# Sample-state products on column quarters and 32-row groups, with attention gates projected ahead of and among sample pairs

## The reference, cut to what matters

```
y_off = einsum('bclgn,bcgrpn,bclgr->bclgrp', cm, h_in, exp(la))      # C x incoming state
states = einsum('bclgn,bclgr,bclgrp->bcgrpn', bm, to_end, xdt)       # B x (decayed x dt)
h = h * chunk_decay + states                                         # new state
out = rms_norm((y_diag + y_off + d_skip * xs) * silu(z_s), norm_g)   # state-space group
o = sum over branches of sigmoid(gate) * branch output
y_att = rms_norm(o * silu(z_a), att_norm_g)                          # attention group
x + gate * (concat(out, y_att) @ w_out), then a final rms_norm
```

## Time and profile before

| what | value |
|---|---|
| median of 3 executions | 985.8 us (982.7 to 985.88) |
| profiled execution, its own time | 985.73 us |
| its span | 983.9 us |
| mean granted TensorE clock | 0.978 |
| TensorE products busy | 924.6 us (94%) |
| VectorE busy | 490.6 us (50%) |
| ScalarE busy | 343.1 us (35%) |
| GpSimd busy | 158.8 us (16%) |
| chain that ended last | PE 77%, DVE 9%, ACT 5%, issue 4%, DMA 4% |

### The profile page before, as it was taken

The page is one execution under the profiler, slowest core; times in us unless marked ns, Lnnn a source line. Parts: engine busy times, 40 slices in busy tenths (PEclk is TensorE's granted clock), DMA queues, the critical chain, the costliest instruction groups (busy, mean ns, idle before and its releaser), DMA issues.

```text
span 983.9 us, 13227 instructions
## 1 busy us (share of the span) xinstructions
PE 924.6 (94%) x5187; PEld 573.6 (58%) x5187; DVE 490.6 (50%) x961; ACT 343.1 (35%) x698; POOL 158.8 (16%) x125
## 2 busy tenths in 40 slices
PE   2999999999999999997989888899999999999995
PEld 1454764465566567776555545556666666666762
DVE  1141301135353445558623445886767666676553
ACT  3140000201011224443132334675665546544531
POOL 1003491000000144435211000900000000000000
PEclk9999999979999989998999999999999999999998
DMA  8926435123120000300832134400000000011011
GB/s 280 352 75 258 171 123 204 44 84 114 57 87 1 5 1 1 86 1 1 310 133 92 47 127 149 129 2 22 12 23 23 22 23 23 1 44 44 1 44 65
DMA packets 36567, 80.67 MB, mean 82 GB/s; under 512 B 3044, under 2 KB 17580, under 8 KB 35162
## 3 DMA queue, kind: packets, MB, share of 16 engines
q1 hardware_dynamic: 32010, 49.39, 15.1%
q0 software_dynamic: 4496, 30.44, 8.6%
HBM read 69.64 MB, written 14.30 MB: 85 GB/s over the span
## 4 chain that ended last, share of the span: by engine, by line
PE 77%; DVE 9%; ACT 5%; issue 4%; DMA 4%; SPq 1%; POOL 0%; ACTq 0%; DVEq 0%
PE PS L1615 12%; PE PS L1554 12%; PE PS L1861 11%; PE PS L1901 7%; PE PS L1924 6%; PE PS L1946 6%; PE PS L1523 3%; PE PS L1597 3%; DMA U<-in_cache_slc_kv,idx 2%; PE PS L1473 1%; PE PS L1783 1%; DMA W<-in_w_ada 1%; PE PS L1558 1%; DVE T L1211 1%; PE PS L1809 1%
## 5 line engine op out<-in xcount | busy, mean ns | idle before, releaser
L1615 PE MATMUL PS<-hT,W 128*128 128x363 f32 (+1 forms) x384 | 119.9, 473 | 0.0
L1597 PE MATMUL PS<-W,hT 128*128 128x512 f32 x256 | 113.0, 594 | 0.0
L977 ACT ACTIVATE T<-PS,small 128x640 f32<-128x640 f32 (+7 forms) x128 | 88.7, 706 | 53.6 <-DVE small L1411 53.3
L1615 PEld LDWEIGHTS PS<-hT,W 128*128 128x128 f32 x384 | 73.2, 192 | 46.6 <-issue 3.0
L1411 DVE TENSOR_REDUCE small<-PS 128x1 f32<-128x640 f32 (+7 forms) x86 | 81.8, 971 | 31.8 <-PE PS L1915 31.3
L1554 PE MATMUL PS<-W,hT 128*128 128x288 f32 (+1 forms) x256 | 86.5, 500 | 0.0
L1924 PEld LDWEIGHTS PS<-consts,T 128*128 128x128 f32 x544 | 60.7, 141 | 35.2 <-issue 32.9
L1924 PE MATMUL PS<-consts,T 128*128 128x128 f32 x544 | 79.6, 276 | 1.5 <-ACT hT L1001 1.5
L1597 PEld LDWEIGHTS PS<-W,hT 128*128 128x128 f32 x256 | 48.2, 191 | 54.7 <-issue 54.1
L1554 PEld LDWEIGHTS PS<-W,hT 128*128 128x128 f32 x256 | 48.5, 190 | 37.4 <-issue 30.7
L1861 PE MATMUL PS<-U,Y 128*128 128x512 f32 x128 | 60.5, 599 | 2.4 <-DVE Q L1434 1.3
(11 more groups left out here) (415 smaller groups left out, 1566.3 us busy)
## 6 DMA issues: line engine op xcount, KB each, us to landing
W<-in_w_in SPq DMA_DIRECT2D x5, 2048.0 KB, 9.1
W<-in_w_ada SPq DMA_DIRECT2D x8, 1024.0 KB, 11.5
U<-in_x_prompt SPq DMA_DIRECT2D x8, 512.0 KB, 8.0
W<-in_w_ada SPq DMA_DIRECT2D x2, 2048.0 KB, 8.0
U<-in_state_win_kv POOLq DMA_DIRECT2D x8, 512.0 KB, 5.0
hT<-in_x_prompt SPq DMA_DIRECT2D x8, 512.0 KB, 3.9
out_y_prompt<-hT SPq DMA_DIRECT2D x8, 512.0 KB, 3.1
out_new_win_sample<-in_state_win_kv POOLq DMA_DIRECT2D x1, 4032.0 KB, 22.2
```

What stands on the lines that cost most here:

```text
L977: ins = act.activation(Pb[u % 4][:, m * step:m * step + n * P], S[:, m, :], ACT.Exp, bias=sneg_m[u % 2][:, m:m + 1], accum_out=dsum[i % 2] ...
L1597: ins = nc.tensor.matmul(bank(z_bank(u)), hT3[:, k, i * P:(i + 1) * P], w, start=(k == 0), stop=(k == KT8 - 1))
L1615: ins = nc.tensor.matmul(bank(b, 0, n), w[:, k, ct % 4 * P:ct % 4 * P + P], hT3[:, k, a:a + n], start=(k == 0), stop=(k == KT8 - 1))
```

## The change: what it does

- `hTs` moves from W to columns 512 to 1023 of U3, scan columns that chunks 4 to 7 have used. The state's turns go in the order `NAT`; ScalarE copies six banks, VectorE two. The gate weights' load waits for chunk 7 alone.
- The state products go to four 32-partition quarters of bank 6, four samples to each accumulation, with 32 columns of `CmT`. VectorE reads the two groups from the two halves of the bank.
- `Bblk` has two tiles in place of four; the new states use 32 rows each (`ind4` masks the samples).
- ScalarE evicts the sample chunk before it squares and gates; GpSimd clears and fills `CmT`, where VectorE did. Decayed states: GpSimd four samples, ScalarE four.
- Units 9 and 10 stand ahead of pair 0, 12, 14 and 16 ahead of pairs 1 to 3, 11, 13, 15 and 17 within the pairs. Results go to other tiles (`za`, `za_s`), unit 10 to bank 6.
- In a pair, small and window scores are computed before the page turns, the pages have a semaphore for each sample, and the Silu of the unit within the pair stands after the copies of the turned probabilities.
- `orow` moves from T to `exs`; the first step of the list no longer waits for its store. `ORDER` is new, with one z (named SAMPLE), which computes nothing on TensorE. The swapped keys `KTx` are copied within the list.

```diff
+    parts["ind4"] = (s[:, None] // NT % 4 == np.arange(4)[None, :]).astype(f)
...
-        Bblk = [b[0:SR] for b in (U3[:, 6, 512:1024], U3[:, 7, 512:1024], xtok[0], KTx[:, 512:1024])]
+        Bblk = [T[0:SR, 0:512], KTx[0:SR, 512:1024]]
...
-        hTs = W[:, 0:4096].rearrange("p (b c) -> p b c", b=NB)
-        STATE_BANK = (1, 2, 3, 4, 7, 0, 5, 6)
+        hTs = U3[:, :, 512:1024]
+        NAT = (0, 1, 2, 3, 4, 6, 5, 7)
+        STATE_BANK = (7, 4, 1, 2, 3, 0, 5, 6)
...
-        orow = T[:, 5376:5568].rearrange("p (n d) -> p n d", n=NBR)
+        orow = exs[:, 0:192].rearrange("p (n d) -> p n d", n=NBR)
...
-        za = W[:, 4096:8192].rearrange("p (i c) -> p i c", i=TT)
+        za = [KTx[:, 512:], KTx[:, 0:512]] + [W[:, 4096 + 512 * i:4608 + 512 * i] for i in range(2, TT)]
+        za_s = hT3[0:SR, :, SEQ:]
...
-        Z_AHEAD, Z_AMID = [[], [10], [12], [14]], [9, 11, 13, 15]
+        Z_AHEAD, Z_AMID = [[9, 10], [12], [14], [16]], [11, 13, 15, 17]
...
+                if i == TT:
+                    pool.wait_ge(s_chunk_done, TT - 1)
+                    nc.gpsimd.memset(T[:, 1024:2048], 0.0).then_inc(s_cm_zeroed, 1)
...
-            for b in range(NB):
-                pool.wait_ge(s_natT, b + 1)
+            pool.wait_ge(s_nat_in, 16 * NB)
+            for b in range(4):
                 nc.gpsimd.tensor_tensor(nat[:, b], nat_in[:, b], edec[:, :, b].unsqueeze(2).broadcast_to([P, 4, P]), ALU.mult).then_inc(s_decayed, 1)
...
-            pool.wait_ge(s_decayed, NB)
-            load_window(0)
-            load_runs(0)
+            pool.wait_ge(s_decayed, 4)
+            pool.wait_ge(s_decayed_act, 16)
+            pool.wait_ge(s_natT, NB)
             pool.wait_ge(s_hout, 1)
             store(pool, O["new_ssm_prompt"][0, 0].rearrange("(c h) d n -> (h d) c n", c=4),
                   hlast.rearrange("p (c n) -> p c n", c=4), s_hstored)
+            pool.wait_ge(s_chunk_done, TT + 1)
+            load_window(0)
+            load_runs(0)
...
-            for i in range(TT):
+            for i in range(TT - 1):
                 ssd_evict(i + 1)
-                if i < TT - 1:
-                    z_square(i)
-                    z_silu(i + 2)
...
+                if i == TT - 2:
+                    ssd_evict(TT)
+                z_square(i)
+                z_silu(i + 2)
...
+            act.wait_ge(s_z_out, 9)
+            for b in range(4, NB):
+                for c in range(4):
+                    act.activation(nat[:, b, c, :], nat_in[:, b, c, :], ACT.Identity, scale=edec[:, c, b:b + 1]).then_inc(s_decayed_act, 1)
...
-                    if n == 1:
-                        z_silu(Z_AMID[p])
-                        act.wait_ge(s_turned, 10 * p + 7)
-                        if p:
-                            act.wait_ge(s_smp_sum, p)
-                        act.activation(PTs[:, 8:12, :].rearrange("p n r -> p (n r)"), bank(4), ACT.Copy).then_inc(s_turned_act, 1)
+                act.wait_ge(s_turned, 10 * p + 7)
+                if p:
+                    act.wait_ge(s_smp_sum, p)
+                act.activation(PTs[:, 8:12, :].rearrange("p n r -> p (n r)"), bank(4), ACT.Copy).then_inc(s_turned_act, 1)
                 act.wait_ge(s_turned, 10 * p + 9)
                 act.activation(PTs[:, 0:4, :].rearrange("p n r -> p (n r)"), bank(0), ACT.Copy).then_inc(s_turned_act, 1)
+                z_silu(Z_AMID[p])
...
-            act.wait_ge(s_orow, 4)
-            act.wait_ge(s_ostored, 64)
...
+                if u == 9:
+                    pe.wait_ge(s_state_added, STATE_BANK.index(7) + 1)
+                if u == 10:
+                    pe.wait_ge(s_state_added, STATE_BANK.index(6) + 1)
...
-                    for g in range(SG):
-                        for b in range(NB):
-                            nc.tensor.matmul(bank(6, g * 256, (g + 1) * 256)[0:SR], CmT[g][:, b * SR:(b + 1) * SR],
-                                             hTs[:, b, g * 256:(g + 1) * 256], start=(b == 0), stop=(b == NB - 1))
+                    for n in range(4):
+                        for q in range(4):
+                            g, m = q // 2, q % 2
+                            b = 4 * m + n
+                            nc.tensor.matmul(bank(6, 0, 256)[32 * q:32 * q + 32], CmT[g][:, b * SR + 32 * m:b * SR + 32 * m + 32],
+                                             hTs[:, b, g * 256:(g + 1) * 256], start=(n == 0), stop=(n == 3))
...
-                nc.tensor.matmul(bank(STATE_BANK[m]), xw[0][0:SR, c * P:(c + 1) * P], Bblk[c // 2 * 2 + h], start=True, stop=True).then_inc(s_state_new, 1)
+                q = slice(32 * h, 32 * h + 32)
+                nc.tensor.matmul(bank(STATE_BANK[m]), xw[0][q, c * P:(c + 1) * P], Bblk[c // 2][q], start=True, stop=True).then_inc(s_state_new, 1)
...
+                    if n in (2, 4):
+                        pe.wait_ge(s_pages[n // 2 - 1], 16 * (p + 1))
...
-                    sp.wait_ge(s_chunk_done, TT + 1)
+                    sp.wait_ge(s_chunk_done, TT)
                     sp.wait_ge(s_ssd_y, TT)
```

More of the change, by code:

```diff
@@ L1718, in _ @@
             pe.wait_ge(s_xtok, 9)
-            for b in range(NB):
+            for b in NAT:
                 if b == 1:
-                    pe.wait_ge(s_decay_cb, 9)
+                    pe.wait_ge(s_cbm, 9)
                 if b == 2:
@@ L1760, in _ @@
                     z_unit(u)
+                queries = [QS[:, 2 * p + b].rearrange("p h t -> p (h t)") for b in range(2)]
                 for n in range(6):
@@ L1764, in _ @@
                     if n == 2:
-                        pe.wait_ge(s_pages, 32 * (p + 1))
+                        if p:
+                            pe.wait_ge(s_smp_read, p)
+                        else:
+                            pe.wait_ge(s_state_added, 8)
+                        for b in range(2):
+                            for o, rhs in ((bank(3, 128, 256), KcTs[:, p // 2 * P:(p // 2 + 1) * P]), (bank(3, 0, 64), KnT[:, 0:SR]),
+                                           (bank(3, 64, 128), KnT[:, SR:])):
+                                ins = nc.tensor.matmul(o[64 * b:64 * b + 64], queries[b], rhs, start=True, stop=True)
@@ new lines, in _ @@
+                        ins.then_inc(s_smp_cscores, 1)
+                        pe.wait_ge(s_turned_act, 5 * p + 1)
+                        pe.wait_ge(s_turned_dve, 5 * p + 1)
+                        for b in range(2):
+                            ins = nc.tensor.matmul(bank(2)[64 * b:64 * b + 64], queries[b], KTwpair[:, b, :], start=True, stop=True)
+                        ins.then_inc(s_smp_wscores, 1)
+                    if n in (2, 4):
+                        pe.wait_ge(s_pages[n // 2 - 1], 16 * (p + 1))
@@ L1775, in _ @@
-                for b in range(2):
-                    for o, rhs in ((bank(3, 128, 256), KcTs[:, p // 2 * P:(p // 2 + 1) * P]), (bank(3, 0, 64), KnT[:, 0:SR]),
-                                   (bank(3, 64, 128), KnT[:, SR:])):
-                        ins = nc.tensor.matmul(o[64 * b:64 * b + 64], queries[b], rhs, start=True, stop=True)
-                ins.then_inc(s_smp_cscores, 1)
-                for n in range(3):
+                for n in range(2):
+                    if n == 0:
+                        pe.wait_ge(s_turned_act, 5 * p + 3)
+                    else:
+                        pe.wait_ge(s_turned_dve, 5 * p + 3)
```

161 lines of the change are left out of this document (85 added, 76 removed).

## The result

The changed kernel took 970.3 us (median of 4 runs, 969.4 to 971.5), the kernel before 985.1 (4 runs, 982.7 to 985.9): a ratio of 0.986, 95% interval 0.984 to 0.988. That is 14.8 us, where 18.8 were forecast. The profiled execution took 970.2, its span is

What follows compares the result with a forecast made beforehand. TensorE's in-order queue and its unfilled waits bound the kernel. Pair 0 starts at 479.6, pairs add 103.4 to 583.0, first score comes at 587.8, the list adds 377.7: span 965.5, time 967, range 959 to 978.

Steps and rivals of the forecast that it cites:

- a list longer than 378 from its first score product: List of steps: a sign that the prediction is wrong; the sum had 377.7 us from there.
- First state turns without a wait, full clock through 450 to 480: Sample state: sign of being right, no wait over 1 us at the first turns; the 3.96 us wait goes.
- State products 2.0, start 457.9; new states 4.0: Sample state: overlapping quarters cut state products from 7.09 to 2.0 us, alternating row groups new states from 7.06 to 4.0.
- no overlap: Rival for the sample state: array parts don't overlap or switching costs as much; 974 us, chance 0.10.
- Units from 465.1 to 465.6, pair 0's turns at 479.6: Units 9 and 10 start when gate weights land (465.1), twice 7.0 us; with 0.5 contention, pair 0 starts 0.4 later.
- the contention: Sample state: GpSimd's clearing and filling of `CmT` may slow VectorE's chunk 6 update; 0.5 us taken.
- A pair 20.8, no page wait: Sample pairs: new order inside a pair saves 2.1 us of 22.9; page wait under 0.3 in pairs 1 to 3.
- Pair 3: Last sample pair: shorter sample unit (3.7 for 7.0), but the top-k chain holds TensorE until 14.7; only 0.8 us gained.
- First score product at 587.8: List start: VectorE's head scaling, key swap and first eviction put it 4.8 us after the stage's end at 583.0.
- List of 377.7 from there: First score to end: 379.6 less 4.8 for unit 17, plus 1.4 late start and 1.5 for less cover and output weights.
- The slower rival: List start: unfilled waits drop the clock and gaps keep it low, doubling product time; 992 us, chance 0.04.
- Output weights, 0.5: List: scaled output weights ready at 627, first output product needs them near 626; 0.5 us added.

Runs made afterwards that it cites:

- e11: Changed kernel with new states' rows 0 to 31 four times, then 32 to 63, plus one useless product in each wait ahead of the state products: 974.1 us.
- e12: Changed kernel with window keys' swap later, first tile's value steps together, and fillers (useless products) in waits of state stage, pair 3 and list start: 966.9 us.

## Why the prediction was right, and where its sizes were off

**Right in kind and sign, 3.3 us short in the time** (967 for 970.3; in the gain 4.0, since the kernel before took 985.1 beside it). Most of its signs of being right came: the state stage, the units back to back, no page wait, pairs of 27.8. One of its signs of being wrong came as well, a list longer than 378 from its first score product: 379.7. By its steps:

- *First state turns without a wait, full clock through 450 to 480.* Held in this trace: the exponential ended at 449.0, as forecast, and the wait of 3.96 went. The clock held here, but less safely than the text said. Eleven of the traces have this kernel's code up to the state products, with the same two waits of 1.23 and 1.04 us. In seven of them the clock was 0.72 over 456 to 462, and the quarter products, 1.93 at the full clock, took 3.25 to 3.5 us in the six of these that have them. So that this trace kept its clock here was luck, of some 1.5 us. With both waits filled (`e11`, `e12`) the clock held both times, which is too few to show that the waits are the cause. The forecast had these waits in its sum as times and not as a risk.
- *State products 2.0, start 457.9; new states 4.0.* 1.93 from 458.09, and 3.87. The changes of form ahead of and behind the quarters cost nothing that the trace shows. The case "no overlap" is out: the experiments show what it would have cost, 5.3 to 6.4 us for the quarters and 3.4 to 6.6 for the row groups, the clock's part with it, which the forecast did not count.
- *Units from 465.1 to 465.6, pair 0's turns at 479.6.* 464.86 and 478.66. Of the 0.9, 0.5 is the contention that I had put on VectorE for GpSimd's clearing of `CmT`. GpSimd's timeline, and VectorE's of the same time:

```profile
443.98 0.95 POOL L732 MEMSET T<- 128x1024 f32 x1
444.99 0.41 POOL L735 COPY T<-U 128x64 f32<-128x64 f32 x2
```

```profile
441.80 2.79 DVE L1237 TENSOR_TENSOR W<-W 128x512 f32<-128x512 f32 x2 [2.57 <-ACT W L915]
444.51 0.68 DVE L1267 TENSOR_TENSOR T<-PS,small 128x512 f32<-128x512 f32 x1
...
445.82 0.69 DVE L1275 TENSOR_TENSOR Y<-Y,T 128x512 f32<-128x512 f32 x1
```

  The clearing and the copies took 1.4 us where the forecast had bounded them by 3.0. The clearing's first 0.6 us lay beside the end of VectorE's second operation of L1237, which has two SBUF inputs; the copies were over before the next such one (L1275, 0.69). VectorE's rows have the durations of the kernel before (2.79, 0.68, 0.69), so the 0.5 was not there. By the rule of the Trainium skill that the prediction weighed (SBUF — State Buffer, SBUF: two separate sides) the sum would have been up to 0.5 lower. The outcome agrees with that, but no operation of VectorE with two SBUF inputs lay beside the clearing or the copies alone for its whole length, so the trace does not test the rule. ScalarE's scalings took 0.30 each (16 in 4.79) where I took 0.35, without effect.
- *A pair 20.8, no page wait.* 478.66 to 499.53 is 20.9, and no page wait is left. The size of the reason was too small. The forecast put 2.1 us on a pair, 8.4 on four; the experiment shows that the inside of the pairs and the page set that lands first are worth 11.4 us together in its trace once the units stand ahead, 9.1 of them waits and the rest mostly products at a lower clock behind them.
- *Pair 3.* This is the first term that was off in this trace: 21.5 us for 20.0. The chain of VectorE and ScalarE was ready 14.95 us after the turns, forecast 14.7, and TensorE's sample unit was done long before, as forecast. But the forecast drew this up as 0.8 us gained and did not write down that the same thing is a wait of 2.0. Behind it the clock falls, and the value sums and what stands with them take 6.58 us, where 5.00 is their time at the full clock. That is the 1.6. It comes and goes: of nine traces with this wait of 2.0 and nothing else changed in pair 3, four lost 1.5 or more here and five took 5.0. With the state stage 0.9 ahead, the pairs end at 583.7 for 583.0.
- *First score product at 587.8.* 588.60. The chain of VectorE operations (1.46, 1.78, 1.4) was in the sum, with 4.8 us for it, and it took 4.9.
- *List of 377.7 from there.* 379.7, the second term that was off, and the one that was off in every trace (378.9 to 381.9 in seven). I had drawn up the 4.8 us between the heads' turn and the first score as time, and not as a wait: 3.83 us without a product, as long as the wait of 3.96 that I had named as the cause of the fall at 455. The slower rival named this very mechanism, and against it stood the longest wait near the list's start, 2.18. That was read in the wrong kernel: unit 16 had covered the place, and the change takes unit 16 away. The rival's price was not reached. In 588.6 to 605 the granted clock has a mean of 0.69, by which 16.4 us hold about 5 us too many of product time (16.4 x 0.31, an estimate), and near 2 of them come back when the wait is filled; with the wait filled the list takes 378.4, within 0.7 of the forecast. Beside the other 3 us TensorE would have waited for ScalarE and VectorE.
- *Output weights, 0.5.* Nothing: GpSimd's scaling ended at 625.6 and the first output product came at 630.07.

For this trace the sum closes: -0.9 for the state stage, +1.5 for pair 3, +0.1 for the first score and +2.0 for the list are 2.7 of the 2.8 us between the spans forecast and measured. Two of these terms are the lot of this one execution: the state stage kept its clock, 1.5 us better than in seven of eleven traces, and pair 3 lost it, 1.5 us worse than in five of nine. The list's term is not luck. What no run took back by itself is the order of ScalarE's eviction of the sample chunk, which took the wait of 3.96 away, and the move of the units to the pairs; these two rest on the traces. What stays open: why behind the same waits the clock falls in some executions and holds in others; and whether the fillers without the moved value steps would come to 965.

## What to carry to other kernels

When a change takes work out of a place, look up the wait that this work had covered, with its length in the new order, and ask what clock the products behind it will get; a rival's condition is to be read in the sum for the new kernel and not in the trace of the old one. Waits of one and two microseconds that look cheap in a sum may cost that much again in slow products, but only as far as no other engine is late anyway: here some 5 us of slow products gave about 2 when they were mended. And joining products so that they overlap gained nothing where VectorE set the pace. One trace is one draw where the clock is near its edge: look at several before a term is booked.

## What the runs showed of the hardware that I had not expected

- Products on 32 rows, four of one row group and then four of the other, ended with the granted clock at 0.50 in both kernels that had this order, with TensorE busy all the time and once with the waits ahead filled. Two row groups alternating (0.24 us a record of 512 columns, against 0.46 on one group at the full clock) kept 1.00 in all eleven traces that had them.
- 32-column quarters with 256 columns in float32 take 0.060 us a record, the same as 64-column halves with 128 columns (0.062).
- Behind waits of 1.23 and 1.04 us, 1.1 us of transposes apart, the clock fell in seven of eleven traces, and in four it held at 1.00. A wait of 2.0 in pair 3 went either way too (four of nine); behind the wait of 3.83 it was low in all nine traces that had it unfilled (the first scores took 1.5 to 1.9 us, 1.08 at the full clock).
